# Block one's projections as three float32r products of split operands, in a ring of six in-place slots, with the modulation chunks spread out

## The reference

```python
x = layer_norm(x, emb_ln_g, emb_ln_b)
for l in range(2):
    # mixer: 30 chunks of 256 columns of w_in
    qa, ka, va, qb, kb, vb, gb, gc, hc, gates = split(x @ w_in[l])     # 7680 columns
    ya, yb, yc = diff_attention(...), neighbourhood_attention(...), gb * dwconv(gc * hc)
    g = sigmoid(gates)
    h = (g0*(ya @ w_branch[l,0]) + g1*(yb @ w_branch[l,1]) + g2*(yc @ w_branch[l,2])) @ w_mix_out[l]
    x = layer_norm(alpha * x + h)
    # attention over a memory of 256 tokens
    q, (k, v) = x @ xa_q[l], split(mem @ xa_kv[l])
    x = layer_norm(alpha * x + (softmax(q k / 16) v) @ xa_o[l])
    x = layer_norm(alpha * x + conv_ffn(x))
# for the second block, from the condition c alone:
mod = silu(c) @ ada_w[l] + ada_b[l]           # 6144 columns a layer
```

## Time and profile before

| | us |
|---|---|
| median of 3 runs (range) | 3275.86 (3271.93 to 3280.26) |
| the profiled execution's own time | 3273.31 |
| its span | 3271.6 |
| TensorE matmul busy | 3013.2 (92%) |
| VectorE busy | 1831.9 (56%) |
| ScalarE busy | 1334.5 (41%) |
| layers of block one, from the first chunk of the first to the first of the second | 26.7 to 787.2 |
| DMA mean rate | 207 GB/s |

### The profile page before, as it was taken

One profiled execution on the slowest core, in us unless ns is written; L12 is line 12 of the kernel. 1 busy time (PEld: TensorE's weight loads), 2 busy tenths in 40 slices (PEclk: granted clock), 3 DMA queues, 4 the chain that ended last, 5 costly groups with the idle time before them and its releaser, 6 DMA issues.

```text
span 3271.6 us, 40332 instructions
## 1 busy us (share of the span) xinstructions
PE 3013.2 (92%) x16564; PEld 2701.6 (83%) x16564; DVE 1831.9 (56%) x1970; ACT 1334.5 (41%) x1451; POOL 28.8 (1%) x68
## 2 busy tenths in 40 slices
PE   7997997998999898898978999979999999999996
PEld 6886886997887687897767997868888898898895
DVE  1275223563255322665354443448888888888885
ACT  0075002331056100333113332217676776777673
POOL 1000000001000000000000000000000000000000
PEclk9998998999999899999979998979999999999998
DMA  9484621546476430555204554218999999999993
GB/s 300 135 283 136 199 78 65 193 154 189 149 232 218 149 128 26 175 173 157 90 26 149 173 179 150 92 34 313 350 352 332 350 360 334 347 356 334 352 353 131
DMA packets 392027, 678.43 MB, mean 207 GB/s; under 512 B 17184, under 2 KB 286528, under 8 KB 391744
## 3 DMA queue, kind: packets, MB, share of 16 engines
q1 hardware_dynamic: 389344, 666.82, 59.1%
q0 software_dynamic: 2528, 9.46, 1.0%
HBM read 675.19 MB, written 4.69 MB: 208 GB/s over the span
## 4 chain that ended last, share of the span: by engine, by line
PE 88%; DVE 7%; ACT 2%; issue 1%; DMA 1%; DVEq 0%; SPq 0%; POOL 0%; ACTq 0%
PE bank L468 87%; DVE ew_lo L1468 1%; DMA ring_head<-in_w_in 1%; PE bank L554 1%; ACT w_hi L1564 1%; PE bank L907 1%; ACT ew_hi L1748 1%; DVE w_lo L1064 0%; DVE std L1013 0%; DVE ka L1169 0%; DVE probs L1059 0%; DVE work L1016 0%; DVE gates L1364 0%; DVE xT L1255 0%; DVE eact_lo L1479 0%
## 5 line engine op out<-in xcount | busy, mean ns | idle before, releaser
L1468 DVE TENSOR_TENSOR ew_lo<-ring_head,ew_hi 128x1792 fp32r<-128x1792 f32 (+2 forms) x384 | 771.5, 2023 | 136.0 <-ACT ew_hi L1748 129.3
L1748 ACT CAST ew_hi<-ring_head 128x1792 fp32r<-128x1792 f32 (+2 forms) x384 | 647.6, 1695 | 279.6 <-PE bank L468 279.6
L1064 DVE TENSOR_TENSOR w_lo<-ring_head,w_hi 128x2048 fp32r<-128x2048 f32 x108 | 247.5, 2292 | 247.9 <-ACT w_hi L1564 247.9
L468 PE MATMUL bank<-x_hi,w_hi 128*128 128x256 f32 x1152 | 332.0, 288 | 13.4 <-DVE w_lo L1064 13.4
L468 PE MATMUL bank<-x_lo,w_hi 128*128 128x256 f32 x1152 | 330.9, 287 | 0.0
L468 PE MATMUL bank<-x_hi,w_lo 128*128 128x256 f32 x1152 | 330.5, 287 | 0.0
L1564 ACT CAST w_hi<-ring_head 128x2048 fp32r<-128x2048 f32 x108 | 205.5, 1903 | 283.4 <-PE bank L468 282.4
L468 PE MATMUL bank<-ew_hi,xe_hi 128*128 128x448 f32 x1024 | 294.9, 369 | 4.4 <-DVE ew_lo L1468 4.4
L468 PE MATMUL bank<-work,ring_head 128*128 128x256 f32 (+1 forms) x1184 | 270.3, 392 | 24.1 <-DVE work L1404 10.9
L468 PE MATMUL bank<-ew_lo,xe_hi 128*128 128x448 f32 x1024 | 291.7, 366 | 0.0
L468 PE MATMUL bank<-ew_hi,xe_lo 128*128 128x448 f32 x1024 | 291.3, 366 | 0.0
(11 more groups left out here) (325 smaller groups left out, 4342.3 us busy)
## 6 DMA issues: line engine op xcount, KB each, us to landing
ring_head<-in_moe_w_gate SPq DMA_DIRECT2D x128, 896.0 KB, 6.5
ring_head<-in_moe_w_up SPq DMA_DIRECT2D x128, 896.0 KB, 6.6
ring_head<-in_moe_w_down SPq DMA_DIRECT2D x96, 1024.0 KB, 7.2
ring_head<-in_w_in SPq DMA_DIRECT2D x56, 1024.0 KB, 5.6
ring_head<-in_ffn_w_in SPq DMA_DIRECT2D x44, 1024.0 KB, 6.6
ring_head<-in_ada_w SPq DMA_DIRECT2D x32, 1024.0 KB, 8.7
ring_tail<-in_w_in SPq DMA_DIRECT2D x26, 1024.0 KB, 6.0
ring_head<-in_ffn_w_out SPq DMA_DIRECT2D x22, 1024.0 KB, 5.3
```

What stands on the lines that cost most here:

```text
L468: ins = nc.tensor.matmul(out, lhsT, rhs, start=start, stop=stop, **kw)
L1064: v.tensor_tensor(w_lo[:, h, :], ring(s), w_hi[:, h, :].bitcast(F32), ALU.subtract).then_inc(w_used[s], 1)
L1468: v.tensor_tensor(ew_lo[:, h, 0:n], ring(c % 6)[:, 0:n], ew_hi[:, h, 0:n].bitcast(F32), ALU.subtract).then_inc(w_used[c % 6], 1)
L1748: a.copy(ew_hi[:, c % DEPTH_HI, 0:n], ring(c % 6)[:, 0:n]).then_inc(f.count(part_hi), 1)
```

## The change

Six things:
1. Every chunk of `w_in`, branches, `w_mix_out`, `xa_kv`, `xa_q` and `xa_o` (62 a layer, numbered i in that order) is split. ScalarE's `high(i)` casts it into one of HI = 3 slots of `w_hi`; VectorE's `low(i)` writes the rest into `ring_low`, which lies over the ring's own slot. `split_features` and `split_tokens` make three float32r matmuls of each product. `high(i)` waits until chunk i-3 is spent (`chunk_spent`), and for the load.
2. The ring has 6 slots, not 9. An `order` written out once gives every chunk its slot; a load waits for the slot's last use, six entries back.
3. The modulation chunks are moved: 0 to 5 among the first 18 chunks (one after each third), 6 to 17 one per step of the loop, 18 and 19 among the mix chunks, 20 to 23 among the `xa_kv` chunks.
4. Activations are split too: xT after its norms, the three branches' inputs (now in the order 2, 1, 0), merged, the memory, and the output of the memory attention. The gates' sigmoid is cut in three.
5. The masked copies `qhalf` go: scores contract over 64 rows. One half of step u+1's scores is issued before the transposes of step u-1.
6. The norm ahead of a layer moves into the loop, behind `high(0)` on ScalarE and `low(0)` on VectorE.

The diff, cut to its core:

```diff
-SLOTS = 9
+SLOTS = 6
+HI = 3
@@ the order of loads and slots
+        order = []
+        for c in range(18):
+            order += [("w_in", c)] + [("ada", c // 3)] * (c % 3 == 2)
+        for u in range(12):
+            order += [("w_in", 18 + u), ("ada", 6 + u)]
+        order += [("branch", 3 * n + b) for n in range(4) for b in (2, 1, 0)]
+        for n in range(4):
+            order += [("mix", n)] + [("ada", 18 + n)] * (n < 2)
+        for n in range(8):
+            order += [("xa_kv", n)] + [("ada", 20 + n)] * (n < 4)
+        order += [("xa_q", n) for n in range(4)] + [("xa_o", n) for n in range(4)]
+        ada_slot = {c: at % SLOTS for at, (kind, c) in enumerate(order) if kind == "ada"}
@@ TensorE
-                    ins.then_inc(f.count(w_used[spent.pop()]), 1)
+                    ins.then_inc(f.count(spent.pop()), 1)
+            def chunk_split(i):
+                k = chunk_cols[i] // CW
+                pe.wait_ge(chunk_lo, f.next(chunk_lo))
+                return tiles(w_hi[:, (i + 2) % HI, 0:k * CW], k), tiles(ring_low[:, chunk_slot[i], 0:k * CW], k), k
+            def chunk_done(i):
+                spent.extend((w_used[chunk_slot[i]], chunk_spent))
+            def split_features(b, i, xh, xl, hi_at=None, lo_at=None):
+                hi, lo, k = chunk_split(i)
+                open_bank(b)
+                for j in range(2):
+                    cols, out = slice(j * P, (j + 1) * P), bank[b][:, j * TOK:(j + 1) * TOK]
+                    for t in range(k):
+                        if hi_at is not None and j == 0 and t % 2 == 0:
+                            pe.wait_ge(hi_at, f.next(hi_at))
+                        mm(out, hi[:, t, cols], xh[:, t, :], t == 0, False)
+                        mm(out, lo[:, t, cols], xh[:, t, :], False, False)
+                    for t in range(k):
+                        if lo_at is not None and j == 0 and t % 2 == 0:
+                            pe.wait_ge(lo_at, f.next(lo_at))
+                        mm(out, hi[:, t, cols], xl[:, t, :], False, t == k - 1, bank_full[b] if (j, t) == (1, k - 1) else None)
+                chunk_done(i)
...
+                        split_features(c % 4, c, x_hi, x_lo)
+                    if c % 3 == 0 and c:
+                        modulation(6, c // 3 - 1)
+                modulation(6, 5)
...
+                score(0, 0)
                 for u in range(18):
                     if u < 16:
+                        score(u, 1)
                     if u < 12:
-                        features(6 + u % 2, xT)
-                        for i in range(2):
-                            modulation(2 + i, 2 * u + i)
+                        split_features(6 + u % 2, 18 + u, x_hi, x_lo)
+                        modulation(2 + u % 2, 6 + u)
+                    if u < 15:
+                        score(u + 1, 0)
                     if 1 <= u <= 16:
                         turn_probs(u - 1, 2 if u - 1 < 8 else 4)
...
                 for n in range(4):
-                    features(n, memT)
+                    split_features(n, 46 + n, mem_hi, mem_lo)
+                    if n:
+                        modulation(6, 19 + n)
                 taken(3)
                 norm_mean()
+                modulation(6, 23)
@@ VectorE
+            def low(i):
+                s, n = chunk_slot[i], chunk_cols[i]
+                dve.wait_ge(chunk_hi, f.next(chunk_hi))
+                v.tensor_tensor(ring_low[:, s, 0:n], ring(s)[:, 0:n], w_hi[:, (i + 2) % HI, 0:n].bitcast(F32), ALU.subtract).then_inc(f.count(chunk_lo), 1)
...
             with f.trips(DEPTH, LAYER1) as l:
+                low(0)
+                norm_centre()
+                norm_finish(eln[:, 0:8], eln[:, 8:16])
+                for q in range(4):
+                    x_low(xT, q)
+                low(1)
+                low(2)
...                                        # chunk c of 18, behind its copy
+                    if c < 17:
+                        low(c + 3)
+                    if c % 3 == 2:
+                        fold(c // 3)
+                    if c % 3 == 0 and c:
+                        folded(6, c // 3 - 1)
+                folded(6, 5)
...                                        # step u, behind peaks(u) and normalise(u - 1)
+                    if u < 13:
+                        low(20 + u)
                     if u < 12:
+                        fold(6 + u)
+                        folded(2 + u % 2, 6 + u)
...                                        # xa_kv chunk n of the first four
                     take(n, (qb, kb)[n // 2][:, 2 * (n % 2):2 * (n % 2) + 2, :])
+                    low(49 + n)
+                    fold(20 + n)
+                    if n:
+                        folded(6, 19 + n)
@@ ScalarE
+            def high(i):
+                s, n = chunk_slot[i], chunk_cols[i]
+                if i >= HI:
+                    eng.wait_ge(chunk_spent, f.next(chunk_spent))
+                eng.wait_ge(w_loaded[s], f.next(w_loaded[s], 16))
+                a.copy(w_hi[:, (i + 2) % HI, 0:n], ring(s)[:, 0:n]).then_inc(f.count(chunk_hi), 1)
...
             with f.trips(DEPTH, LAYER1):
+                high(0)
+                norm(eps1, yT, centred)
+                x_casts()
+                high(1)
+                high(2)
...
+                for c in range(3, 20):
+                    high(c)
+                    if c % 3 == 2:
+                        modulate(c // 3 - 1)
+                modulate(5)
+                modulate(6)
                 for u in range(18):
                     if u < 16:
                         exps(u)
+                    if u < 13:
+                        high(20 + u)
                     if u < 11:
-                        modulate(2 * u + 2)
+                        modulate(7 + u)
                     if u < 12:
                         take(6 + u % 2, gates[:, 2 * u:2 * u + 2, :])
...
+                for n in range(4):
+                    modulate(20 + n)
+                    high(49 + n)
```

More of the change, by code:

```diff
@@ L1101, in _ @@
                     b, i = c % 4, c % 2
-                    if c in (6, 7):
-                        dve.wait_ge(bank_full[b], f.next(bank_full[b]))
-                        for m in range(2):
-                            v.tensor_scalar(qhalf[1][m][:, 2 * i:2 * i + 2, :], pairs(b), half[m], None, ALU.mult).then_inc(f.count(bank_free[b] if m else vector_step), 1)
-                    elif c in (4, 5, 10, 11):
+                    if c in (4, 5, 10, 11):
                         take(b, (va if c < 6 else vb)[:, :, i * CW:(i + 1) * CW])
                     else:
-                        take(b, (qa, ka, None, None, kb, None, gb, gc, hc)[c // 2][:, 2 * i:2 * i + 2, :])
+                        take(b, (qa, ka, None, qb, kb, None, gb, gc, hc)[c // 2][:, 2 * i:2 * i + 2, :])
                     if c == 7:
@@ L1174, in _ @@
+                f.bump(bank_full[6], 6)
+                f.bump(bank_free[6], 6)
                 for n in range(4):
[L1175 to L1176 removed]
+                    for i, br in enumerate((2, 1, 0)):
+                        c = 3 * n + i
                         b = c % 4
+                        if n == 0:
+                            dve.wait_ge(gates_ready, f.next(gates_ready))
                         dve.wait_ge(bank_full[b], f.next(bank_full[b]))
@@ L1564, in split_high, with cast, x_casts, norm @@
                 a.copy(w_hi[:, h, :], ring(s)).then_inc(f.count(hi_ready[h]), 1)
-            def norm(eps, src, before, dense=False):
+            def high(i):
[4 more added lines that the diff above has]
+                a.copy(w_hi[:, (i + 2) % HI, 0:n], ring(s)[:, 0:n]).then_inc(f.count(chunk_hi), 1)
+            def cast(dst, x, ready, done):
+                eng.wait_ge(ready, f.next(ready))
+                a.copy(dst, x).then_inc(f.count(done), 1)
+            def x_casts():
+                for q in range(4):
+                    ks = slice(2 * q, 2 * q + 2)
+                    cast(x_hi[:, ks, :], xT[:, ks, :], x_pieces if q < 3 else x_ready, x_hi_ready)
+            def norm(eps, src, before, dense=False, meanwhile=lambda: None):
                 a.preload_act_table(ACT.Sqrt)
@@ L1665, in _ @@
                 eng.wait_ge(f.last, f.now(f.last))
-                a.activation(flat, flat, ACT.Sigmoid).then_inc(f.count(gates_ready), 1)
-                norm(eps1, yT, centred)
+                for i in range(2):
+                    h = slice(2 * i, 2 * i + 2)
+                    cast(x_hi[:, h, :], qa[:, h, :], branch_in, branch_hi)
+                for i in range(3):
+                    g = flat[:, (2 - i) * CH:(3 - i) * CH]
+                    a.activation(g, g, ACT.Sigmoid).then_inc(f.count(gates_ready), 1)
+                    high(33 + i)
+                for n in range(4):
+                    h = slice(2 * n, 2 * n + 2)
+                    cast(merged_hi[:, h, :], merged[:, h, :], merged_in, merged_cast)
+                    for i in range(3 if n < 3 else 0):
```

(26 more changed lines are left out.)

266 lines of the change are left out of this document (162 added, 104 removed), and 22 rows, old and new, of the table LAYER1.

## The result

| | before | after | forecast |
|---|---|---|---|
| median (range), us | 3273.89 (3271.02 to 3280.26), 4 runs | 3395.28 (3390.74 to 3401.21), 4 runs | 3368 (3305 to 3425) |
| ratio, 95% interval | | 1.0366 (1.0350 to 1.0382): slower | slower |
| span of the profiled execution | 3271.6 | 3389.1 | |
| granted TensorE clock, mean | 0.954 | 0.916 | |

A forecast was written before the change was run, and what follows sets the result against it. TensorE's rate was taken to bound the chunks, short VectorE and ScalarE chains the rest. Terms of +38.4 a layer, 76.8 for two, plus 17.6 for first chunks gave +94.4 on 3273.3: 3368 us, range 3305 to 3425.

The forecast's parts named there:

- The loop: Loop of 12 steps: slot, load, cast, low part, fold, modulation in a chain; steps average 13.0 us, +27 a layer.
- Rival 2: The clock stays at 1.2 GHz in the loop: 15.3 us a step, 3418 us in all; chance 13%.
- The 18 chunks: First 18 chunks: faster matmuls against five stalls of 1.9 us, added modulations and some clock loss; +2 a layer.
- The first chunk: Layer one's start: the norm waits behind chunk 0's load, cast and low part; +15.8 us.
- Mix, kv and q: Mix, xa_kv and xa_q chunks: folds behind low parts that wait for loads stall modulations; +15 us a layer.
- Branches: Twelve half chunks of the branches get faster despite a cold start, and the wait for qa goes; -6.7 us a layer.
- Tail: Loop's tail: low(32), memory casts and the low part of hc land between short chains; +1.5 us a layer.
- Attention over the memory and xa_o: Late low(60) +3.1 and split output +0.7, against 4.6 us saved on four xa_o chunks; -0.8 a layer.
- Feed-forward part and boundaries at 0: Feed-forward part and block two keep their work: 0; start of layer two +1.8 us for splitting xT.
- With six slots: In the loop, chunk 20+u's load waits until chunk 17+u, which held its ring slot, is spent.
- Rival 1: TensorE stays the bound, loads and splits running ahead of modulations: loop steps of 8.9 us, 3198 in all; chance 12%.
- Rival 3: Stalls are smaller: loop steps of 12.3 us without clock loss, 3337 in all; no separate chance given.

The follow-up runs named there:

- run 1: Changed kernel with VectorE's fold(6+u) put ahead of low(20+u) in the loop's steps; 3308.3 us.
- run 2: Changed kernel with VectorE's fold put ahead of the low part among the mix chunks and first four xa_kv chunks only; 3370.1 us.
- run 3: Changed kernel with the norm's mean on TensorE issued at a layer's end and once ahead of the loop over layers; 3392.5 us.
- run 6: Changed kernel with the norm put back outside the loop over layers on all three engines, ahead of high(0) and low(0); 3395.2 us.
- run 4: Changed kernel with high(0) and low(0) put behind the norm they stood ahead of; 3397.9 us.
- run 5: Changed kernel with run 1, run 2 and, among the 18 chunks, modulate ahead of high and fold ahead of low; 3253.82 us, 0.9933 of the kernel before.
- run 9: Kernel of run 5 with every chunk's ring slot turned on by four; 3240.7 us.
- run 12: Kernel before the change with a ring of six slots in place of nine and nothing else; 3290.9 us.

## Why the prediction was right, and where it was not

- **The loop** (forecast +27, measured +23.5 and, in the second layer, +28.9): right in mechanism, event by event, and shown by run 1. Steps took 12.6 in the first layer, where fewer had the late exponentials, and 13.0 in the second, as forecast. The clock is not free here either. The chain runs through TensorE's scores, and the same loop takes 150.7 at a granted clock of 0.82, 155.4 at 0.79 in the second layer, 154.7 to 155.1 at 0.78 to 0.79 in runs 2, 3 and 6, and 158.2 at 0.77 in run 4. Rival 2, 15.3 a step throughout, didn't come, but single steps of 15.2 did (run 4).
- **The 18 chunks** (+2, +2.1): stalls of 1.7 ahead of each modulation for the 1.9 forecast. Turned round in run 5.
- **The first chunk** (+15.8, +16.4): the cast ahead of the norm did what the sum said. But the 16 us are not what another order gives back: run 4 won 12 of them and had lost them by the mix chunks, 4 among the 18 chunks, where a load shows, and 8 in the loop.
- **Mix, kv and q** (+15, +21.5): the largest miss. The waits were forecast at 29.6 (4.6 at the start, 0.9, 6.5, 9, 6.4 and 2.2) and came to 24.5 (5.4, 0.7, 6.1, 7.9, 4.4 and 0). What was mis-sized is the clock: 0.7 taken, while TensorE is busy 117.0 us for work put at 105.1, at a granted clock of 0.87. That is 12 us a layer. And the chain there had a link that the prediction didn't name: modulations 21 and 22 wait for the copy of the modulation before. It ends with the fold, so the sum didn't show it, but turning the fold round left it in place (run 2).
- **Branches** (-6.7, -7.7): 288 matmuls in 36.0, with a cold start: the first ones 0.21 apart, the later ones 0.119, and a granted clock of 0.67 in the first 5 us. That VectorE might fall behind was named: it didn't hold TensorE up here, but it was over 3 us late at the end, and that is part of the wait in the first mix chunk. The 109 ns of the Trainium skill ("TensorE: Matmul & The Clock Gate", "Wait — 56ns, not 53.3ns?"), weighed in the prediction, aren't reached here either.
- **Tail** (+1.5, +3.9): its clock of 0.55 against 0.63 goes with it; not taken apart further.
- **Attention over the memory and xa_o**: together 0.7 less than forecast in layer one, 1.3 more in layer two.
- **Feed-forward part and boundaries at 0** failed in two places. "With six slots" was followed for the loop and not for the stage behind xa_o, where the first load's slot is that of the last chunk: +2.7 (run 9 gives it back). And the norm behind the loop's back edge meets a wait of 4.9 that no row of before shows, since nothing waited there: +6.4 in all for 1.8. Run 3 takes 5.2 of it away, and run 6 shows the like on VectorE. That it is the fetch of code is an inference: the profile names nothing.
- **The total**: over two layers the clock in mix to q (23), the norms ahead of the feed-forward parts (5), the boundary (5) and the tail (4) were forecast too low by 37; the waits in mix to q (10), the branches (4) and the loop (2) too high by 16. The small terms left give 2 more. The miss is 23 of 117.5: the sum was helped by terms that cancel.
- **Rival 1** is what runs 1 and 5 made real: with the chain under TensorE's work, steps of mostly 8.3 to 9.4, near its 8.9. It was priced at 3198, and the kernel with the orders turned takes 3254, since the kv waits, the first chunk and the boundary stay. **Rival 3** (no clock loss) fell with the clock in the loop and in mix to q.

What stays open: how much of the 8 us a layer that six slots cost the kernel before (run 12) is in the changed kernel too; what the wait behind the back edge is; why the granted clock differs between runs of the same stage; and whether the waits of the kv part go when the copy of a modulation is put ahead of the low part, with the loads as they are.

## What to carry to other kernels

When an engine gets a new task, look at what stands behind it in that engine's own order: here 4.2 us of VectorE and ScalarE work a chunk fitted into their idle time, and where it stood cost 137 us (3389.1 against 3252.2), because it was put ahead of short pieces that TensorE waited for. Write down, for each wait of the bound engine, the releasing instruction and all that is ahead of it in its queue, loads included; two exchanged lines were worth 82 us. And an engine's idle time inside a chain over other engines isn't free room: work put there lengthens the chain. When an edit should shorten one stage, read that stage: run 3 hit its 5 us there, and the total, with a loop 4 us longer at a lower clock, hid it.

## What was not expected of the hardware

- **The granted clock falls between near-identical kernels at different places.** In run 5 it was 0.50, the level of 1.2 GHz, for 225 to 230 of the loop, while TensorE was busy all 5 us; it had been at 0.96, busy 4.7 of 5, just before, with one wait of 0.32. The step took 12.9. In run 9, with other slots and the same work, it was 1.00 there and that step took 9.2; but it was 0.67 at 215 to 220, in a step of 9.9, and there it fell with TensorE busy throughout 200 to 220. What decides isn't shown. In order, 220 to 225 and 225 to 230 of run 5, then 215 to 220 and 225 to 230 of run 9:

```profile
220.00:225.00 5.00, 4.68 (x32) 3.92 (x32) 4.89 (x6) 5.00 (x10) 0.00 (x0) 0.96 0.54 167
225.00:230.00 5.00, 5.00 (x19) 3.70 (x18) 4.49 (x12) 2.06 (x7) 0.00 (x0) 0.50 1.04 351
```

```profile
215.00:220.00 5.00, 5.00 (x31) 5.00 (x31) 4.75 (x11) 3.30 (x8) 0.00 (x0) 0.67 1.09 363
...
225.00:230.00 5.00, 5.00 (x40) 4.67 (x40) 4.79 (x11) 1.82 (x5) 0.00 (x0) 1.00 1.03 350
```

  Over the whole loop run 5 takes 111.9 at 0.93 and run 9 108.1 at 0.96. So differences of 4 us between two such kernels may be the clock's, and not the edit's.
- **Behind a loop's back edge** the first engine that is needed waits 2 to 5 us with nothing named (4.94 on TensorE, 3.54 and 2.12 or 2.20 on VectorE). Moving the work to the other side moves the wait to another engine (runs 3 and 6), and it costs little where that engine's wait lies beside other work: 0.8 in run 3.
